# A first norm without loops, and expert products in three fp32r parts

## What is computed

```python
u = rms_norm(h, norm1_w)            # h: 1040 x 1024
...
def expert_block(args):
    xblk, e = args                  # xblk: 128 x 1024
    hid = silu(xblk @ w_gate[e]) * (xblk @ w_up[e])   # 1024 -> 512
    return hid @ w_down[e]                            # 512 -> 1024
```

## Time and profile before

| | |
|---|---|
| median of the runs | 4067.8 us |
| the profiled execution | 4042.96 us, span 4041.3 us |
| PE matmul busy | 3377.1 us, 84% |
| DVE busy | 1507.2 us, 37% |
| ACT busy | 1075.8 us, 27% |
| POOL busy | 302.7 us, 7% |
| granted PE clock, mean | 0.911 |
| DMA | 418.38 MB, 104 GB/s on average |

### The profile page before, as it was taken

One profiled execution on the slowest core, in us unless ns is written; L12 is line 12 of the kernel. 1 busy time (PEld: TensorE's weight loads), 2 busy tenths in 40 slices (PEclk: granted clock), 3 DMA queues, 4 the chain that ended last, 5 costly groups with the idle time before them and its releaser, 6 DMA issues. The chain is left out here.

```text
span 4041.3 us, 54716 instructions
## 1 busy us (share of the span) xinstructions
PE 3377.1 (84%) x20137; PEld 2631.2 (65%) x20138; DVE 1507.2 (37%) x2642; ACT 1075.8 (27%) x2239; POOL 302.7 (7%) x338
## 2 busy tenths in 40 slices
PE   2999978889677764998998998996998479999992
PEld 1999976667344443888888888885777434444441
DVE  3111113330555655656656656655432200000002
ACT  3111112221444432433433433433321111111110
POOL 0000002220000002001101001101000110000001
PEclk9999989989888986998988998987998689999996
DMA  2322222111211101000000000000532458888884
GB/s 86 139 94 94 89 91 84 42 65 39 59 31 35 42 9 47 2 24 18 7 24 18 7 24 18 7 24 24 154 120 90 167 208 335 323 340 329 339 317 177
DMA packets 153541, 418.38 MB, mean 104 GB/s; under 512 B 14146, under 2 KB 95044, under 8 KB 141060
## 3 DMA queue, kind: packets, MB, share of 16 engines
q1 hardware_dynamic: 119248, 330.28, 22.7%
q10 hardware_dynamic: 25620, 60.39, 4.0%
q0 software_dynamic: 8480, 25.22, 1.8%
HBM read 334.92 MB, written 80.92 MB: 103 GB/s over the span
## 5 line engine op out<-in xcount | busy, mean ns | idle before, releaser
L565 PE MATMUL at_S<-at_k,at_q 128*104 128x512 f32 (+10 forms) x544 | 201.5, 491 | 34.7 <-DMA at_v<-s_v 19.3
L2080 PE MATMUL ex_bank<-wd,ex_hT 128*128 128x512 f32 x512 | 227.7, 597 | 1.4 <-ACT ex_hT L2123 1.4
L2056 PE MATMUL ex_bank<-wgu,ex_xT 128*128 128x512 f32 x512 | 226.9, 596 | 0.0
L236 PE MATMUL pf_acc<-uH,pf_wH 128*128 128x260 f32 x1344 | 216.3, 282 | 12.2 <-DVE pf_wL L254 12.2
L2064 PE MATMUL ex_bank<-wgu,ex_xT 128*128 128x512 f32 x512 | 224.9, 592 | 0.0
L345 PE MATMUL ph_acc<-ph_wH,uH 128*104 128x512 f32 x480 | 196.0, 408 | 26.1 <-DVE ph_wL L356 26.1
L236 PE MATMUL pf_acc<-uH,pf_wL 128*128 128x260 f32 x1344 | 217.2, 284 | 0.0
L236 PE MATMUL pf_acc<-uL,pf_wH 128*128 128x260 f32 x1344 | 216.4, 283 | 0.0
L236 PEld LDWEIGHTS pf_acc<-uH,pf_wH 128*128 128x128 f32 x1344 | 185.3, 189 | 12.5 <-issue 12.5
L2129 DVE COPY ex_y<-ex_bank 128x512 f32<-128x512 f32 x32 | 22.1, 692 | 457.7 <-PE ex_bank L2080 457.7
L345 PE MATMUL ph_acc<-ph_wL,uH 128*104 128x512 f32 x480 | 192.6, 401 | 0.0
(11 more groups left out here) (362 smaller groups left out, 7131.3 us busy)
## 6 DMA issues: line engine op xcount, KB each, us to landing
wgu<-in_expert_w_gate SPq DMA_DIRECT2D x32, 2048.0 KB, 13.2
wgu<-in_expert_w_up SPq DMA_DIRECT2D x32, 2048.0 KB
wd<-in_expert_w_down SPq DMA_DIRECT2D x32, 2048.0 KB, 8.3
pf_w<-in_w_in SPq DMA_DIRECT2D x44, 512.0 KB
s_pT<-pf_ev ACTq DMA_DIRECT2D x42, 520.0 KB, 2.6
s_y<-ex_y ACTq DMA_DIRECT2D x32, 512.0 KB, 11.0
rw_x<-s_pT SPq DMA_DIRECT2D x29, 520.0 KB, 4.8
ph_w<-in_w_in SPq DMA_DIRECT2D x6, 2048.0 KB
```

The lines of the kernel that those rows point to most:

```text
L236: last = nc.tensor.matmul(acc[:, s, n, 0:CW], ww[:, s, k, :], uu[:, k, n * CW:(n + 1) * CW], start=(k == 0 and j == 0), stop=(k == KD - 1 ...
L565: last = nc.tensor.matmul(S[n][:, lo:hi], q[:, s, n, t * TT:(t + 1) * TT], k[:, s, lo:hi], start=True, stop=True)
L2056: last = nc.tensor.matmul(bank[:, GATE_BANK[s], :], xT[:, s, k, :], wgu[:, s, 0, k, :], start=(k == 0), stop=(k == KD - 1))
L2080: last = nc.tensor.matmul(bank[:, 5 + o, :], hT[:, k, :], wd[:, s, k, o * 512:(o + 1) * 512], start=(k == 0), stop=(k == FK - 1))
```

## The change

`norm1` is written without loops. All ten tiles of x have their own place in `h` (`[TT, NT, D]`), and SP issues all their loads at once, with the weights of the norm spread over 104 partitions. DVE scales a tile by the reciprocal and by the weights in one scalar_tensor_tensor, in place, before it is turned. What PE turns is then already u; ACT rounds it straight from PSUM, and DVE subtracts from PSUM. `pt` has four places. ACT and DVE prepare tile t+2 before they finish tile t.

In `experts` every operand of a product is split. ACT casts the weights to `wH` (fp32r) in halves of 2048 columns per partition, and DVE subtracts for `wL`; both have two places, which the products use in turn, by `rank` (the order of the products: G0, U0, G1, D0, U1, G2, D1, ...). A half of a place may be overwritten when PE has used it (`w_used`). SP loads the next weights when both low halves of a matrix are made (`w_low`), no longer when PE is done with it. The turned x and the turned hidden tile are split too (`xTH`, `xTL`, `hTH`, `hTL`). y leaves PSUM in one copy of 1024 columns on ACT. PE's order of steps is as before. Each product runs in two halves, each with a wait of its own for `w_low`, and `project` takes k outside and the two output halves inside.

```diff
 def norm1(nc, c):
+            for t in range(1, NT):
+                sp.dma_start(h[:, t, :], c.x[0, t * TT - META:(t + 1) * TT - META, :]).then_inc(h_in[t], 16)
...
-                    nc.vector.tensor_scalar(u[:, s, :], h[:, s, :], ri[:, s:s + 1], None, ALU.mult).then_inc(u_done, 1)
...
-                    for b in range(2):
-                        nc.vector.tensor_tensor(
-                            v[:, s, 4 * b:4 * b + 4, :], pt[:, s, b, 0:4 * TT].rearrange("p (k t) -> p k t", k=4),
-                            w[:, 4 * b:4 * b + 4].unsqueeze(2).to_broadcast([128, 4, TT]), ALU.mult).then_inc(scaled, 1)
...
+            def normed(t):
+                dve.wait_ge(rs_done, t + 1 + OPEN)
+                nc.vector.reciprocal(ri[:, t:t + 1], rs[:, t:t + 1]).then_inc(ri_done, 1)
+                dve.wait_ge(ri_done, t + 1 + OPEN)
+                nc.vector.scalar_tensor_tensor(out=h[:, t, :], in0=h[:, t, :], scalar=ri[:, t:t + 1], in1=w[:],
+                                               op0=ALU.mult, op1=ALU.mult).then_inc(u_done, 1)
+
+            normed(0)
+            normed(1)
+            for t in range(NT):
+                if t + 2 < NT:
+                    normed(t + 2)
+                dve.wait_ge(high, t + 1 + OPEN)
+                nc.vector.tensor_tensor(wide(c.uL, t), turned(t), wide(c.uH, t), ALU.subtract).then_inc(low, 1)
...
 def experts(nc, c):
+            def reload(j, s, n, r):
+                sp.wait_ge(w_low, 2 * r + 2 + OPEN)
+                load(sp, j, s, n + 2)
...
+        def three(out, aH, aL, bH, bL, first, last):
+            nc.tensor.matmul(out, aH, bH, start=first, stop=False)
+            nc.tensor.matmul(out, aL, bH, start=False, stop=False)
+            return nc.tensor.matmul(out, aH, bL, start=False, stop=last)
...
+        def into_hidden(pe, out, s, r, w):
+            for h in range(2):
+                pe.wait_ge(w_low, 2 * r + h + 1 + OPEN)
+                for k in range(4 * h, 4 * h + 4):
+                    last = three(out, xTH[:, s, k, :], xTL[:, s, k, :], wH[:, w, k * FF:(k + 1) * FF],
+                                 wL[:, w, k * FF:(k + 1) * FF], k == 0, k == KD - 1)
+                last.then_inc(w_used, 1)
...
-            for k in range(KD):
-                last = nc.tensor.matmul(bank[:, GATE_BANK[s], :], xT[:, s, k, :], wgu[:, s, 0, k, :],
-                                        start=(k == 0), stop=(k == KD - 1))
...
+        def project(pe, n, r, w):
+            pe.wait_ge(h_low, n + 1 + OPEN)
+            pe.wait_ge(y_moved, n + OPEN)
...
+                    split(U, 1 - s, 0, rank(U, n + 1), s, i + s)
+                    move_h(n)
+                    split(U, 1 - s, 1, rank(U, n + 1), s, i + s)
+                    open_gate(1 - s, n + 1, rank(G, n + 1))
+                    move_x(s, n + 2)
+                    for h in range(2):
+                        split(G, s, h, rank(G, n + 2), 1 - s, i + 1)
+                    move_y(s, n, i, rank(DN, n))
+                    for h in range(2):
+                        split(DN, 1 - s, h, rank(DN, n + 1), s, i + s)
...
+            def low(j, s, h, r, w):
+                dve.wait_ge(w_high, 2 * r + h + 1 + OPEN)
+                part = slice(h * HALF, (h + 1) * HALF)
+                nc.vector.tensor_tensor(wL[:, w, part], raw(j, s)[:, part], wH[:, w, part], ALU.subtract).then_inc(w_low, 1)
...
+                    low_h(n)
+                    for h in range(2):
+                        low(U, 1 - s, h, rank(U, n + 1), s)
+                    low_x(s, n + 2)
+                    for h in range(2):
+                        low(G, s, h, rank(G, n + 2), 1 - s)
+                    low(DN, 1 - s, 0, rank(DN, n + 1), s)
+                    mix(1 - s, n + 1, rank(U, n + 1))
+                    low(DN, 1 - s, 1, rank(DN, n + 1), s)
```

More of the change, by code:

```diff
@@ L99, in norm1 @@
         sb, ps, sem, begin = scope(nc, st)
[L100 removed]
+        h = sb("n1_h", [TT, NT, D])
         sq = sb("n1_sq", [TT, D])
[L102 to L108, removed]
[L109 to L110 removed]
@@ L111, in norm1 @@
[L111 to L119, removed]
+        ms = sb("n1_ms", [TT, NT])
+        rs = sb("n1_rs", [TT, NT])
+        ri = sb("n1_ri", [TT, NT])
+        w = sb("n1_w", [TT, D])
+        pt = ps("n1_pt", [128, 4, 2, 512])
+        w_in = sem("n1_w_in")
@@ L134, in _, with spread @@
+            for t in range(1, NT):
+                sp.dma_start(h[:, t, :], c.x[0, t * TT - META:(t + 1) * TT - META, :]).then_inc(h_in[t], 16)
         @block.scalar
         def _(act):
[L136 to L146, removed]
+            def spread(t):
+                act.wait_ge(h_in[t], (32 if t == 0 else 16) + OPEN)
+                nc.scalar.activation(sq[:], h[:, t, :], ACT.Square, accum_out=ms[:, t:t + 1]).then_inc(sq_done, 1)
+                act.wait_ge(sq_done, t + 1 + OPEN)
+                nc.scalar.activation(rs[:, t:t + 1], ms[:, t:t + 1], ACT.Sqrt, bias=c.eps[0:TT, :], scale=1.0 / D).then_inc(rs_done, 1)
@@ L2108, in _ @@
                 with pe.If_ne(used, 0):
-                    for step in (turn_x, gate, up, turn_h, project):
-                        step(pe, 0, n + NE, n + NE // 2)
-        def move_x(act, s, n):
-            act.wait_ge(x_turned, n + 1 + OPEN)
-            nc.scalar.copy(xT[:, s].rearrange("p (b k) t -> p b (k t)", b=2), bank[:, 0:2, :]).then_inc(x_moved, 1)
-        def open_gate(act, s, n):
-            act.wait_ge(gate_done, n + 1 + OPEN)
-            act.wait_ge(mixed, n + OPEN)
-            nc.scalar.activation(sg[:], bank[:, GATE_BANK[s], :], ACT.Sigmoid).then_inc(opened, 1)
@@ L2121, in move_h @@
[L2121 to L2134 removed]
+                    r = ORANK + 3 * n
@@ L2136, in _, with high @@
+                    turn_x(pe, 0, n + NE, n + NE // 2)
+                    gate(pe, 0, n + NE, r, 0)
+                    up(pe, 0, n + NE, r + 1, 1)
+                    turn_h(pe, n + NE)
+                    project(pe, n + NE, r + 2, 0)
         @block.scalar
         def _(act):
-            move_x(act, 0, 0)
-            move_x(act, 1, 1)
-            open_gate(act, 0, 0)
+            def high(j, s, h, r, w, times, free):
+                act.wait_ge(w_in[j][s], 16 * times + OPEN)
+                act.wait_ge(w_used, free + OPEN)
+                part = slice(h * HALF, (h + 1) * HALF)
+                nc.scalar.copy(wH[:, w, part], raw(j, s)[:, part]).then_inc(w_high, 1)
@@ L2193, in _ @@
                 with dve.If_ne(used, 0):
-                    mix(dve, 0, n + NE)
-                    move_y(dve, 0, n + NE, n + NE // 2, 1)
+                    r = ORANK + 3 * n
+                    low_x(0, n + NE)
+                    for j in range(3):
+                        for h in range(2):
+                            low(j, 0, h, r + j, j % 2)
+                    mix(0, n + NE, r + 1)
+                    low_h(n + NE)
 def combine(nc, c):
```

297 lines of the change are left out of this document (170 added, 127 removed).

## The result

| | before | after |
|---|---|---|
| median of the runs, same chip | 4066.7 us (4064.1 to 4070.1, four) | 3912.7 us (3896.6 to 3924.6, four) |
| the profiled execution | 4042.96 us, span 4041.3 | 3896.57 us, span 3894.9 |
| PE busy | 3377.1 us | 3250.0 us |
| DVE busy | 1507.2 us | 1964.3 us |
| ACT busy | 1075.8 us | 1434.1 us |

The ratio of the times is 0.962 [0.957, 0.966]: 154 us gained where 137 were forecast, or 146.4 from profiled execution to profiled execution. Three instructions mark the borders between what the change touches and what it doesn't. The timeline of the kernel before has (start, duration, idle time ahead in brackets)

What follows compares the result with a forecast made beforehand. PE was taken to bound the experts (22.07 us each), a chain of waits the first norm. Norm -46, periods -92, gathers +2, ends -1 give -137: 4067.8 - 137 = 3931 us, 8-in-10 range 3914 to 3970.

Steps and rivals of the forecast that it cites:

- first norm: First norm's ten tiles: shorter chain, two table loads instead of ten, ending at 39.4 us against 85.7: -46 us (-50 to -36).
- 30 periods: Expert loop: PE's period falls from 22.07 to 19.0 us, three products of 5.6 plus 2.2, for 30 experts: -92 us.
- late gathers: Expert stage: gathers for even experts have 1 us to spare instead of 4; +2 us in all for those coming late.
- ends of the stage: Before and behind the expert loop: cheaper products against the first split and DVE's last work in a row: -1 us.
- the pace of fp32r matmuls: Expert products: 72 fp32r matmuls at the merge's 0.2333 us each, 16.8 us per expert for 20.6.
- The 0.4 us for reciprocal and handoffs: First norm, per tile on DVE: added to 2.31 us for a one-column reciprocal and three handoffs, making 2.7 us.
- The splits: Experts' weight halves of 2048 columns: 1.90 us per cast on ACT, 2.29 us per subtraction on DVE, six each per expert.
- DVE as the bound: Rival in the experts: POOL's DMAs or handoffs stretch DVE's 17.5 us to 19 to 20: +30, 3961 us; chance 0.13.
- The 18 us from a turn to the next rows: Even experts' gathers: about 1.7 + 0.58 + 3.5 + 12.2 us from turn_x to data, in a period of 19.0.
- the rival of the text: Gather sets every second expert: data after 20 to 21 us, even steps 1 to 2 us longer: +30, 3961 us; chance 0.15.
- Transfers: Rival in the experts: at 345 GB/s, 7.34 MB take 21.3 us per expert: +69, 4000 us; chance 0.04.
- a share of 0.95: Expert stage: a sign of being right, the DMA engines' busy share at about 0.95.

Runs made afterwards that it cites:

- e_both: The changed kernel, but project begins with matmuls on the high part of h and even experts' gathers are issued one turn earlier: 3860.2 us, ratio 0.951.
- e_high_first: The changed kernel, but project begins with the eight matmuls needing only the high part of h and waits for the low part behind them: 3919.9 us, ratio 0.965.
- e_norm: The kernel before with the new first norm alone, its experts unchanged: 4017.1 us for 4059.8, ratio 0.989.
- e_small_store: The changed kernel, but each expert stores 128 of its result's 1024 columns, the rest of the buffer being zeroed beforehand: one execution, 3967.1 us.
- e_lowh_late: The changed kernel, but DVE takes the low part of h behind the first low half of the up weights, not ahead of it: 3967.4 us, ratio 0.978.

## Why the prediction was right or wrong

The sum by its own terms, from profiled execution to profiled execution:

| term | forecast | measured |
|---|---|---|
| first norm | -46 | -47.6 |
| 30 periods | 30 x (19.0 - 22.07) = -92 | 30 x (18.58 - 22.07) = -104.7 |
| late gathers | +2 | +6.3 |
| ends of the stage | -1 | -2.2 |
| unchanged stages between | 0 | +3.5 |
| combine | 0 | -1.7 |
| sum | -137 | -146.4 |

- **The mechanism held in both parts.** In the norm two table loads are left, DVE sets the pace, and from its third tile to its last but one it waits for nothing. In the experts PE's products and the turn set the period. `project` starts 2.12 us after turn_h where 2.2 were worked out, and moving only this wait, later or away, moves the median period from 18.57 to 19.95 or 17.85 us.
- **The step that failed is the pace of fp32r matmuls** in the term of the 30 periods, "42 steps, 0.2333 us each". The path was right and its largest part was sized too long. In the experts L2046, the first of three, starts at 3439.62 and again, two threes later, at 3440.98: 1.36 us for six, 0.227 each. From the start of `project` to the next turn_h the 72 take 18.57 - 2.12 = 16.45 us, where 16.8 stood. That is 0.35 of the 0.42 us by which the period was too long; the other 0.08 is the handoff. Over 30 experts the pace is 10.5 us of the 12.7 that the term missed. The number to take was in the same trace. The output stage of the kernel before, with the same helper and shape, shows at full granted clock

```profile
3070.07 0.39 PE L1394 MATMUL or_bank<-wideH,or_mH 128*128 128x512 f32 x1
...
3070.75 0.39 PE L1394 MATMUL or_bank<-wideH,or_mH 128*128 128x512 f32 x1
```

  which is three matmuls in 0.68 us. I read one stage only, took its pace as that of the form, and gave no bound below it. Why the merge runs at 0.233 stays open. It is no stall now and then: its steps are 0.231, 0.232 and 0.237 us, over and over, at a granted clock of 1.00. That other engines are busy doesn't explain it: in the experts DVE and ACT are busy for 0.89 and 0.76 of the time, at 0.227.
- **A tile of the norm takes 2.33 us and not 2.7**: the reciprocals start at 18.78 and 21.11. Its three instructions last 2.45 us in the rows, more than the pace, since the next starts before the last one's recorded end (20.18 is 1.21 after 18.97, with a duration of 1.28). The 0.4 us for reciprocal and handoffs were not there to be paid. A first subtraction that began at 17.85 us, where its end was forecast at 17.7, took some of it back.
- **The splits fit as drawn**, to 0.01 us an instruction. DVE had more room than worked out: 89.47 us busy of 100 are 16.6 us per expert and not 17.5, and in `e_both` the same work fits into 17.85 us with DVE idle for 8% of it. The chance of 0.13 for DVE as the bound was spent on POOL's DMAs stopping DVE. The subtractions show nothing of that, with 2.285 us in the mean; the hold goes the other way, from the subtractions to POOL's gathers.
- **The late gather is real, but not as told.** It was to cost 1 to 2 us in every second expert. In the changed kernel's two profiles it costs nothing in most periods and 3.9 to 6.5 us in one and in three of them. The 18 us from a turn to the next rows came out about right by luck, from two errors that cancel. In the 11 shorter waits of `e_high_first` (up to 1.5 us) the token numbers took 5.9 to 6.5 us where 3.5 were put in, and the rows were there 9.8 to 11.1 us after their issue where 12.2 were. So the rows did not come later with fuller engines, as the prediction had argued; the token numbers did. Where a gather was late by far, both were long, 7.2 and 14.5 us in the case above, and POOL's own instruction, taken at 0.98 us, was stretched to 2.97 beside DVE's subtraction. A part of each long case is the clock behind the wait, for which the prediction had no term. With the shorter period of `e_high_first` the gather does become the rival of the text, in every second expert.
- **Transfers are not the bound**: the row of 442 GB/s was the right one to trust, since 414 were held over 100 us. The Trainium skill, SBUF — State Buffer, "A bandwidth-pool intuition that's wrong", names some 358 GB/s; the rows of this case are above that, and they decide. The forecast of a share of 0.95 was not far off from 0.98 and 0.99, and that share said little: it stands at 1.00 in the faster kernel.
- **The range ended at 3914, 1.3 us above the median.** Of the 18.1 us between the sum (3930.8) and the median (3912.7), 9.4 are in the terms above. The other 8.7 are no part of the mechanism: the median before stood 24.8 us above the profiled execution and the median after only 16.2. The range allowed for no period under 19.0, and for nothing for the unchanged stages, which alone move a median by more than 1.3 us. With either of the two right it would have held, so where the median fell beside its end is chance; that the period was 0.42 us too long is not. Its upper side was full of rivals, each with a reason; the lower side had none, because the best row for the largest term had been taken as exact.

## What to carry to other kernels

Where the largest term is a count times a pace, read that pace in every stage of the trace that has the form, and put the spread into the range on both sides. A resource that is busy for 0.99 of the time is no bound until something that needs less of it, or more, has been tried: here the kernel with a share of 1.00 was the faster one. When a step of an engine gets shorter, look for the requests that were timed by its old length; here one line that asks earlier for a gather was worth no more than the late gathers of that execution (0 to 16 us) while the path was long, and was needed for the next 24 us of the stage. When a wait of PE grows, look at the granted clock behind it before pricing the wait alone.

## What the runs showed of the hardware that was not expected

The unchanged stages vary from execution to execution by more than the terms that were argued over. The line L926 of the RWKV stage (in the kernel before, L938), first and last start, in the kernel before, in the changed one, and in `e_norm`, in this order:

```profile
L938 PE MATMUL rw_bank<-rw_kr,rw_bkz x640: 337/339/672, 1582.4 to 2758.1; 128*104 128x208 f32 x160
```

```profile
L926 PE MATMUL rw_bank<-rw_kr,rw_bkz x640: 337/340/671, 1535.3 to 2713.3; 128*104 128x208 f32 x160
```

```profile
L926 PE MATMUL rw_bank<-rw_kr,rw_bkz x640: 337/339/671, 1541.8 to 2735.7; 128*104 128x208 f32 x160
```

That is 1175.7, 1178.0 and 1193.9 us for the same code. Over the nine profiled executions other than that of `e_small_store` the RWKV stage took 1306.5 to 1330.8 us and attention 495.3 to 505.5, with a mean granted clock of 0.898 to 0.911 over the whole span. The projections, the merge and the output stage agreed within 3 us. The granted clock goes with the length: in attention it is 0.89 where the stage took 495 to 496 us and 0.86 where it took 505, and in RWKV 0.88 where it took 1306 to 1313 us and 0.86 at 1330.8, while the busy times of DVE and ACT differ by under 3 us. No run changed the clock alone, so that it is the cause was not tried. In the experts it is 1.00 in the long stretches shown for the changed kernel and `e_both`, and 0.52 in the short ones behind a wait of PE; in `e_lowh_late` the same wait of 1.95 us is followed by it in one period of three only, and what decides that stays open.

The transfers are the other thing: one core held 392, 401 and 414 GB/s over 100 us each. A small read beside them is slow as well as uneven: POOL waited 3.5 us in the mean for 512 bytes of token numbers before, 7.0 in the changed kernel, and up to 13.4 in `e_high_first`. And a subtraction on DVE with both inputs in SBUF holds a gather's instruction on POOL: 23 of 32 in the changed kernel and 29 of 32 in `e_both` started beside one and ended 0.85 to 0.86 us after it, whatever was left of it, up to 3.0 us in all; the longest of the others is 1.02, with some beside a subtraction from PSUM among them.
